# Half of expert 0's bias and the count of tokens, moved behind its first product and its second chunk

## The reference

```python
logits = tok @ router_w + router_b
topv, topi = lax.top_k(logits, 4)
combine = sum(one_hot(topi, 32) * softmax(topv)[..., None], axis=1)
for e in range(32):
    gu = tok @ w1[e] + b1[e]                      # 1024 -> 2048
    gate = minimum(gu[:, :1024], 7.0)
    lin = clip(gu[:, 1024:], -7.0, 7.0)
    act = (lin + 1) * gate * sigmoid(1.702 * gate)
    out = out + combine[:, e:e + 1] * (act @ w2[e] + b2[e])
```

## Time and profile before

| what | value |
|---|---|
| median of 3 runs | 1093.72 us |
| the profiled execution's own time | 1094.23 us |
| its span, first to last instruction | 1092.5 us |
| TensorE busy | 1059.1 us (97%) |
| VectorE, ScalarE, GpSimd busy | 283.4, 174.7, 47.0 us |
| moved by DMA | 432.57 MB, 396 GB/s over the span |
| mean granted TensorE clock | 0.997 of full speed |

### The profile page before, as it was taken

The page is one execution under the profiler, slowest core; times in us unless marked ns, Lnnn a source line. Parts: engine busy times, 40 slices in busy tenths (PEclk is TensorE's granted clock), DMA queues, the critical chain, the costliest instruction groups (busy, mean ns, idle before and its releaser), DMA issues.

```text
span 1092.5 us, 11750 instructions
## 1 busy us (share of the span) xinstructions
PE 1059.1 (97%) x4858; PEld 407.9 (37%) x4858; DVE 283.4 (26%) x574; ACT 174.7 (16%) x385; POOL 47.0 (4%) x38
## 2 busy tenths in 40 slices
PE   9999999999999999999999999999999999999998
PEld 7455446333333333333333333333333333333332
DVE  4986575211111111111111111111111111111111
ACT  3253313011111111111111111111110111111112
POOL 0637000000000000000000000000000000000000
PEclk9999999999999999999999999999999999999999
DMA  9933589899999999999999999999999999999996
GB/s 340 363 126 126 229 331 378 355 426 429 421 418 426 434 429 433 428 433 431 432 432 426 437 432 431 433 431 431 432 431 433 431 433 428 436 428 434 425 428 263
DMA packets 34602, 432.57 MB, mean 396 GB/s; under 512 B 3580, under 2 KB 5136, under 8 KB 17680
## 3 DMA queue, kind: packets, MB, share of 16 engines
q1 hardware_dynamic: 32384, 430.73, 93.5%
q10 hardware_dynamic: 2192, 1.48, 0.5%
HBM read 431.15 MB, written 1.05 MB: 396 GB/s over the span
## 4 chain that ended last, share of the span: by engine, by line
PE 66%; DMA 33%; DVE 0%; issue 0%; SPq 0%; POOL 0%; POOLq 0%; DVEq 0%
DMA ring<-in_expert_w_dram 33%; PE bank L473 24%; PE bank L502 14%; PE bank L1575 13%; PE bank L511 4%; PE bank L436 3%; PE bank L463 2%; PE bank L450 1%; PE bank L485 1%; PE bank L455 1%; PE bank L1541 0%; PE bank L443 0%; PE bank L1796 0%; PE bank L1523 0%; PE bank L1546 0%; PE bank L1533 0%
## 5 line engine op out<-in xcount | busy, mean ns | idle before, releaser
L473 PE MATMUL bank<-ring,work 128*64 128x512 f32 x2048 | 453.5, 598 | 16.6 <-DMA ring<-in_expert_w_dram 16.6
L473 PEld LDWEIGHTS bank<-ring,work 128*64 128x64 f32 x2048 | 143.6, 138 | 322.9 <-issue 289.5
L502 PE MATMUL bank<-ring,work 128*64 128x512 f32 x992 | 219.4, 593 | 10.4 <-DMA ring<-in_expert_w_dram 10.3
L1415 DVE TENSOR_SCALAR work<-bank 128x512 f32<-128x512 f32 x31 | 21.4, 691 | 462.1 <-PE bank L473 462.1
L502 PEld LDWEIGHTS bank<-ring,work 128*64 128x64 f32 x992 | 74.5, 137 | 150.4 <-issue 148.1
L1575 PE MATMUL bank<-ring 128*128 128x512 f32 x224 | 99.1, 596 | 0.0
L984 ACT ACTIVATE work<-work 128x512 f32<-128x512 f32 x31 | 19.5, 630 | 484.8 <-DVE work L1415 484.8
L537 DVE TENSOR_TENSOR work<-bank,vecs 128x512 f32<-128x512 f32 x31 | 21.4, 691 | 211.1 <-PE bank L450 211.1
L511 PE MATMUL bank<-work,putT 64*128 64x512 f32 x248 | 61.9, 616 | 0.0
L1575 PEld LDWEIGHTS bank<-ring 128*128 128x128 f32 x224 | 41.7, 190 | 49.0 <-issue 48.6
L436 PE MATMUL bank<-xs,pick 128*64 128x512 f32 x248 | 58.5, 593 | 0.0
(11 more groups left out here) (251 smaller groups left out, 521.8 us busy)
## 6 DMA issues: line engine op xcount, KB each, us to landing
ring<-in_expert_w_dram SPq DMA_DIRECT2D x70, 4096.0 KB, 39.5
ring<-in_expert_w_dram SPq DMA_DIRECT2D x41, 2048.0 KB, 14.7
ring<-in_expert_w_dram SPq DMA_DIRECT2D x17, 1024.0 KB, 9.7
ring<-in_w_in_dram SPq DMA_DIRECT2D x8, 2048.0 KB, 21.2
ring<-in_w_out_dram SPq DMA_DIRECT2D x2, 2048.0 KB, 10.3
ring<-in_w_branch_attn_dram SPq DMA_DIRECT2D x1, 2048.0 KB, 8.0
ring<-in_w_branch_pool_dram SPq DMA_DIRECT2D x1, 2048.0 KB, 12.8
work<-in_expert_w_dram SPq DMA_DIRECT2D x2, 1024.0 KB, 10.0
```

Source lines behind the costliest of these rows:

```text
L473: mm = pe.matmul(dst, hTe[:, at:at + SLOTS], w[a][:, col:col + BANK], start=(k == 0 and not bias_first), stop=(k == KD - 1 and bias_first) ...
L502: mm = pe.matmul(ps[SLOTS * half:SLOTS * (half + 1), :], actT[:, at:at + SLOTS], w[a // 2][:, col:col + BANK], start=(k == 0), stop=(k == ...
L1415: nc.vector.tensor_scalar(gate_e, ps_gate[:, :], SWIGLU_LIMIT, None, ALU.min).then_inc(gate_ok, 1)
```

## The change

The two quarters of expert 0's bias that go to `ps_gate` (0 and 1) stay in front. The two that go to `ps_lin` (2 and 3) are written after the last chunk of expert 0, before `gemm1` is raised; `start` and `stop` of the products are set per quarter to fit. `count_tokens` moves from behind the gather to behind expert 0's chunk 1. Since `bias_pick` is still read after chunk 3, VectorE's copy for expert 1 moves behind expert 0's gated unit. The order of the gather stays.

```diff
-        def up_bias(pe, first=True):
-            for q in range(4):
+        def up_bias(pe, first=True, quarters_of=range(4)):
+            for q in quarters_of:
...
-        def up(pe, w, c, rows=range(W1_ROWS), bias_first=True):
+        def up(pe, w, c, rows=range(W1_ROWS), bias_first=range(4)):
...
-                                   start=(k == 0 and not bias_first), stop=(k == KD - 1 and bias_first), skip_group_check=True)
+                                   start=(k == 0 and q not in bias_first), stop=(k == KD - 1 and q in bias_first), skip_group_check=True)
...
             build_put(slot_id, 0).then_inc(put_ok, 1)
-            build_bias_pick(1).then_inc(s["bias_ok"], 1)
...
                 glu(e, wide)
                 if first:
+                    build_bias_pick(1).then_inc(s["bias_ok"], 1)
                     rows_in(1, gain_at)
...
             pe.wait_ge(s["bias_ok"], 1)
-            up_bias(pe)
+            up_bias(pe, True, range(0, 2))
...
             gather_first(pe, 1, 1).then_inc(rowsT_ps, 1)
-            count_tokens()
...
-                    mm = up_early(w, c)
+                    mm = up_early(w, c, bias_first=range(0, 2))
                     if c < W1_CHUNKS - 1:
                         mm.then_inc(chunk_used, 1)
-                mm.then_inc(gemm1, 1)
+                    if c == 1:
+                        count_tokens()
+                up_bias(pe, False, range(2, 4)).then_inc(gemm1, 1)
```

More of the change, by code:

```diff
@@ L1916, in _, with up_early @@
             gather_first(pe, 1, 1).then_inc(rowsT_ps, 1)
-            count_tokens()
-            def up_early(w, c):
-                up(pe, w, c, range(0, 1)).then_inc(half_used, 1)
-                return up(pe, w, c, range(1, W1_ROWS))
+            def up_early(w, c, bias_first=range(4)):
+                up(pe, w, c, range(0, 1), bias_first).then_inc(half_used, 1)
+                return up(pe, w, c, range(1, W1_ROWS), bias_first)
             def down_early(w, c):
```

## The result

The change makes the kernel slower by 0.47%: 1099.68 us against 1093.53 us (medians of 9 runs each; ratio 1.0047, 95% interval 1.0035 to 1.0058). That is 5.1 us by the ratio, where 2.3 were forecast and 1096.0 us named. The medians themselves lie 6.15 us apart, since the median of a kernel with two kinds of runs sits in the larger group.

What follows compares the result with a forecast made beforehand. TensorE sets the weight stream until 328 us, then the stream sets the end. A 2.6 us delay less 0.3 hidden gives 2.3, so 1096.0 us against a median of 1093.72; range 1093.8 to 1097.0.

Steps and rivals of the forecast that it cites:

- (a): Front bias at 186.07 us: taking out two of four products running side by side saves 0, bounds 0 and 0.51 us.
- (b) to (e): TensorE from expert 0 to expert 1: start 0.20 us earlier, count 0.38, end bias 1.11, copy wait; expert 1 2.6 late.
- rival 2: Bias products don't share the array in pairs only: end 1.3 us later, 1095.0, or 1096.7 in costly form; chance 0.08.
- (f): Weight stream, loads issued at 307.97 and 328.05 us: of 2.6 us delay 0.3 is hidden, 2.3 reach the end.
- Rival 1: Loads of 308 and 328 us: the queue gives back up to 2.2 us, leaving +0.4, 1094.1 us; chance 0.14.
- Rival 3: Stream never waits for TensorE after 194 us: end 0.2 to 0.7 us earlier, 1093.0 to 1093.5; chance 0.06.

Runs made afterwards that it cites:

- e5: The change with all four bias products in front and VectorE's copy ahead of expert 0's gated unit; 1094.66 us, ratio 1.001.
- e11: The change with VectorE's copy ahead of expert 0's gated unit, two bias products still in front; 1099.46 us, ratio 1.0055.
- e1: The change with all four bias products in front again, two of them overwritten; 1095.6 us, ratio 1.0021.
- e4: The kernel before with only the count of tokens moved behind expert 0's second chunk; 1093.94 us, ratio 1.0005.
- e6: The kernel before with the tokens of expert 3 gathered twice, at 252 us, ahead of the late loads; 1094.38 us, ratio 1.0008.
- e3: The kernel before with only VectorE's copy of expert 1's bias moved behind expert 0's gated unit; 1093.83 us, ratio 1.0005.
- e7: The kernel before with the tokens of expert 6 gathered twice, at about 360 us, behind the late loads; 1093.72 us, ratio 1.0002.
- e8: The kernel before with two additions of x1 moved from 264 and 292 us to 318 and 345 us; 1091.99 us, ratio 0.9985.
- e2: The change with the count of tokens back in front, bias still split and copy still late; 1100.55 us, ratio 1.006.
- e9: The kernel before with bias quarters 2 and 3 moved behind gather and count, and VectorE's copy ahead of the gated unit; 1098.98 us, ratio 1.0057.
- e10: The kernel before with all four bias quarters behind gather and count, and VectorE's copy ahead of the gated unit; 1098.76 us, ratio 1.0044.

## Why the prediction was wrong

The sign and the first mechanism were right; the size was not.

**(a), the front bias.** The time of the step was right: 1.01 us for two products against 1.02 for four, so 0 saved. But the step took what the two products do for the time as all that they do, and its bounds, 0 and 0.51, reckoned only with a gain. This is the step that failed. Two products that cost no time were needed to keep TensorE's clock up. Every later duration was taken from the earlier trace rows at full clock, and no rival asked whether the clock would stay. The loss is 4.7 us by the rows, 4.7 between the two groups of runs of the change, and 4.8 by e5 and e11. The earlier trace rows begin at 186 us and don't show what TensorE does ahead of the bias. The trace of before has small products from 178 us on, two of the rows being

```profile
178.80 1.99 PE L1796 MATMUL bank<-ring,xn 128*128 128x256 f32 x8
...
184.83 1.31 PE L1821 MATMUL bank<-rw,work 128*128 128x32 f32 x10
```

That the clock would fall there without the two products no row said, and no run here shows what in this stretch it depends on. A bound for a loss was missing all the same.

**(b) to (e), TensorE's lateness.** Read on e1, where the clock stays up, moved to the front of the earlier trace rows:

| step | predicted | measured |
|---|---|---|
| product of expert 0 starts earlier | 0.20 | 0.19 |
| gather of expert 1 starts later | 1.3 | 206.24 + 0.36 - 205.21 = 1.39 |
| wait for the copy | over 1 | 1.16 |
| count between chunks 1 and 2 | 0.38 | 0.48, in e4 |
| end bias, with its way in | 1.11 | 206.24 - 190.87 = 15.37, less 14.27 in e4: 1.10 |
| expert 1's bias later | 2.6 | 209.70 - 207.02 = 2.68 |
| expert 1's product later | 2.6 | 212.24 - 209.57 = 2.67 |

The count came out 0.03 us over its upper bound of 0.45, which changes nothing. The four bias products that run side by side are borne out too, and with them the rejection of rival 2: a pair at the end costs 206.24 - 205.24 = 1.00 us, not 0.5 and not 1.7.

**(f), the stream.** Until the load of 328 us TensorE sets the stream. How much of a delay reaches the end:

| run | delay on TensorE before 308 us | at the end, by the ratio |
|---|---|---|
| e1 | +2.68 | +2.3 (1.3 to 3.3) |
| e6 | +1.71 | +0.9 (-0.1 to 1.9) |
| e5 | +1.44 | +1.1 (0.1 to 2.1) |
| e3 | +1.37 | +0.5 (-0.4 to 1.5) |
| e4 | +0.28 | +0.5 (-0.4 to 1.5) |
| e7 | 0.0 (1.7 later on) | +0.2 (-0.8 to 1.2) |
| e8 | -1.73 | -1.6 (-2.6 to -0.7) |

The forecast of 2.3 out of 2.6 is what e1 shows; with an interval of 1.3 to 3.3, that it agrees to the tenth is chance. By the middle values 0.3 to 0.9 us of each delay over 1 us are given back where 0.3 were put, but every interval of e1, e3, e5, e6 and e8 also holds the whole delay. Rival 1, the queue absorbs it, is refuted at its far end: e1 is clear of its +0.4 us. Whether more than the 0.4 us that it needs is given back, the times don't decide; that some is, the landings suggest (2.5 and 2.0 us late in e1, 1.9 and 1.1 in e6). Rival 3 is refuted by e1 and e8. Of the three parts of the change, the count alone (e4) and the copy alone (e3) do nothing that can be measured, and the halved bias carries the loss: its missing half in front lowers the clock, its half at the end costs TensorE 1.1 us, and it forces the copy to wait.

What stays open: why the clock falls in about half of the runs of the change (5 of 9) and of e2 (4 of 6), but in all runs of e9, e10 and e11; and whether less than two products could be taken from the front without a fall. Where the clock falls in time is known from one profiled execution each of the change, e9, e10 and e11; for the other runs it is inferred from their mean clock. What decides it inside the chip, no run here shows.

## What to carry to other kernels

Before work is taken out of TensorE's queue because it runs beside other work for nothing, ask whether the clock will stay up without it: look at the clock of every run and not only at the median, and put a price on a fall (here 4.7 us). When a stream of loads sets the end, find the last issue that comes too late for the queue; work moved from in front of it to behind it was won almost whole (e8, by the middle value), and a delay in front of it counts however busy the stream is afterwards (e1). A tile shared by consecutive steps turns a later read into a later refill: the wait appears on the engine that wants the refill, here 1.16 us.

## What had not been expected of the hardware

- The granted clock fell to 0.50 with TensorE busy 2.00 of 2.00 us before the fall and 10.00 of 10.00 in it (the change and e9). It fell at about 188 us in the change and e11, at 188 to 189 in e9, and somewhat earlier in e10 (0.84 over 186 to 188, where TensorE also idles 0.79 us), and stayed down for some 10 us in each.
- Two fp32 products of 512 columns on 32 rows each take 1.00 to 1.01 us, four side by side 1.02. The two that cost nothing in time make the difference for the clock: 22 of 22 runs at 0.996 or more with them (e1, e5), 5 of 5 at 0.994 or less (e11) and 5 of 9 at 0.993 or less (the change) without.
